# Column-tiled modulation matmuls: four narrow ones per weight row block, or one of 512 columns

## The reference

```python
silu_c = jax.nn.silu(c)            # (1, 1024)
silu_cc = jax.nn.silu(c_ctx)       # (1024,)
for layer in range(DEPTH):         # DEPTH = 2, N_MOD = 6, D = 1024
    mod = (silu_c @ w_mod[layer] + b_mod[layer])[:, None, :]
    mod_c = silu_cc @ w_mod[layer] + b_mod[layer]
    shift1, scale1, gate1, shift2, scale2, gate2 = jnp.split(mod, N_MOD, axis=-1)
```

## Time and profile before

| | before |
|---|---|
| median of 3 runs (lowest, highest) | 2513.5 us (2512.9, 2515.27) |
| the profiled execution's own time | 2513.5 us |
| its span in the profile | 2511.7 us |
| granted TensorE clock, mean share of full speed | 0.996 |
| PE busy | 2447.8 us, 97% |
| ACT busy | 1239.9 us, 49% |
| records of the mod matmuls | 1536 matmuls, 1536 weight loads |
| records of the turns | 24 matmuls, 24 weight loads |

### The profile page before, as it was taken

How to read it: one execution, slowest core, us unless ns; L and a number is a source line. 1 busy time by engine, 2 the same in 40 slices (tenths; PEclk the granted TensorE clock), 3 DMA queues, 4 the chain that set the end, 5 groups by cost and what they waited for, 6 DMA issues and landing times.

```text
span 2511.7 us, 43973 instructions
## 1 busy us (share of the span) xinstructions
PE 2447.8 (97%) x17556; PEld 2170.5 (86%) x17556; DVE 1159.2 (46%) x2116; ACT 1239.9 (49%) x2133; POOL 1462.1 (58%) x853
## 2 busy tenths in 40 slices
PE   7999999999999999999999999999999999999998
PEld 7998889999999889999677877778888878899998
DVE  8896645443978554527426522221001023535144
ACT  6458554455447764446544522453323345636543
POOL 6875747457976755556442334645565546564970
PEclk9999999999999999999999999999999999999999
DMA  6544343345544443346321112232222223245554
GB/s 244 185 168 166 121 168 142 145 185 188 184 168 166 152 174 129 135 156 222 147 71 63 52 68 88 84 117 88 97 101 84 101 107 129 85 152 185 185 185 151
DMA packets 50607, 347.73 MB, mean 138 GB/s; under 512 B 5361, under 2 KB 8689, under 8 KB 8945
## 3 DMA queue, kind: packets, MB, share of 16 engines
q1 hardware_dynamic: 47840, 340.31, 37.3%
q10 hardware_dynamic: 2576, 4.72, 0.6%
HBM read 343.96 MB, written 1.05 MB: 137 GB/s over the span
## 4 chain that ended last, share of the span: by engine, by line
PE 85%; ACT 5%; DVE 4%; POOL 3%; issue 1%; DMA 1%; ACTq 0%; DVEq 0%; SPq 0%; POOLq 0%
PE pg L1951 23%; PE pg L1953 22%; PE pg L1952 22%; POOL ring_lo L668 2%; ACT ring_hi L797 2%; PE ps L2272 2%; PE ps L2293 2%; PE ps L2291 1%; PE ps L2428 1%; PE ps L2409 1%; PE ps L2122 1%; DMA ring<-in_w_stream_dram 1%; PE ps L2128 1%; PE ps L2509 1%; PE ps L2502 1%
## 5 line engine op out<-in xcount | busy, mean ns | idle before, releaser
L668 POOL TENSOR_TENSOR ring_lo<-ring,ring_hi 128x1024 fp32r<-128x1024 f32 (+3 forms) x502 | 1171.2, 2348 | 683.4 <-ACT ring_hi L797 682.7
L1951 PE MATMUL pg<-HH,ring_hi 128*128 128x256 f32 (+1 forms) x3264 | 1036.0, 317 | 15.0 <-POOL ring_lo L668 8.6
L1952 PE MATMUL pg<-HH,ring_lo 128*128 128x256 f32 (+1 forms) x3264 | 989.6, 303 | 0.0
L1953 PE MATMUL pg<-HL,ring_hi 128*128 128x256 f32 (+1 forms) x3008 | 917.7, 305 | 0.0
L1951 PEld LDWEIGHTS pg<-HH,ring_hi 128*128 128x128 f32 x3264 | 616.4, 189 | 72.5 <-issue 33.9
L1952 PEld LDWEIGHTS pg<-HH,ring_lo 128*128 128x128 f32 x3264 | 616.6, 189 | 42.4 <-issue 15.5
L1953 PEld LDWEIGHTS pg<-HL,ring_hi 128*128 128x128 f32 x3008 | 567.7, 189 | 28.1
L797 ACT ACTIVATE ring_hi<-ring 128x1024 fp32r<-128x1024 f32 (+3 forms) x572 | 563.8, 1002 | 35.4 <-DMA ring<-in_w_stream_dram 34.3
L807 ACT ACTIVATE take<-pg 128x256 f32<-128x256 f32 (+1 forms) x242 | 103.7, 429 | 427.2 <-PE pg L1953 421.1
L1953 PE MATMUL pg<-big_r,ring_hi 128*128 128x256 f32 (+1 forms) x928 | 299.4, 323 | 0.0
L1951 PE MATMUL pg<-big_r,ring_hi 128*128 128x256 f32 (+1 forms) x752 | 246.1, 327 | 3.9 <-DVE ring_lo L1637 2.7
(11 more groups left out here) (346 smaller groups left out, 3295.3 us busy)
## 6 DMA issues: line engine op xcount, KB each, us to landing
ring<-in_w_stream_dram SPq DMA_DIRECT2D x320, 1024.0 KB, 4.8
hn<-in_consts_dram ACTq DMA_DIRECT2D x2, 1024.0 KB, 5.8
cst<-in_consts_dram SPq DMA_DIRECT2D x1, 1472.0 KB, 19.9
prm<-in_params_dram SPq DMA_DIRECT2D x1, 1110.0 KB, 9.4
X<-in_xT_dram SPq DMA_DIRECT2D x1, 1024.0 KB, 5.8
X<-in_ctxT_dram ACTq DMA_DIRECT2D x1, 1024.0 KB, 6.4
out_dram<-H ACTq DMA_DIRECT2D x4, 256.0 KB, 2.2
cst<-in_consts_dram SPq DMA_DIRECT2D x1, 768.0 KB, 16.9
```

Of the source, the lines that this page charges most:

```text
L668: pool.tensor_tensor(ring_lo[:, slot, cols], ring[:, slot, cols], ring_hi[:, place * P:(place + n) * P].bitcast(F32), SUB).then_inc(sem(LO ...
L1951: first = pe.matmul(out, a[0], b[0], start=start, stop=False)
L1952: pe.matmul(out, a[1], b[0], start=False, stop=False)
L1953: return first, pe.matmul(out, a[0], b[1], start=False, stop=stop)
```

## The change

Each block of a mod chunk becomes one matmul of 512 columns instead of four of 128. Block c goes to output partitions 32 (c mod 4) and up, so each of the four groups of array columns sums two of the eight blocks, and the sum over the groups is left open. ACT copies the whole 128x512 bank to `mod_rows`. The turn becomes four float32 matmuls, each with 128 columns of `mod_rows` as stationary operand and a new 128x2 constant `sel` as moving operand, which has a one wherever the partition modulo 32 is 0 (first column) or 1 (second column): it sums the four groups and turns the rows at once, so ACT then drains 8 adjoining columns. `n_parts`, `ORDER`, the gaps, the banks and the rings stay as they are. `sel` adds two columns to the early constants.

```diff
+    c["sel"] = (i[:, None] % MOD_COLS == np.arange(2)[None, :]) * 1.0
...
-           "ident": P, "ones": P, "eps6": 1, "eps5": 1, "half_pi": 1, "lam_init": DEPTH, "inv1": 1,
+           "ident": P, "ones": P, "eps6": 1, "eps5": 1, "half_pi": 1, "lam_init": DEPTH, "inv1": 1, "sel": 2,
...
@@ drain_fill (ACT)
-                        act.activation(mod_rows[:, i % 2, 0:P], ready(CHUNK[name, l, i])[:, 0:P], ACT.Copy).then_inc(sem("drained"), 1)
+                        act.activation(mod_rows[:, i % 2, :], ready(CHUNK[name, l, i]), ACT.Copy).then_inc(sem("drained"), 1)
                     elif name == "modt":
-                        columns = ready(CHUNK[name, l, i])[:, 0:P].rearrange("p (a n) -> p a n", a=MOD_TILES)
-                        act.activation(mod[:, l, 4 * i:4 * i + 4, :], columns[:, :, 0:2], ACT.Copy).then_inc(sem("drained"), 1)
+                        drain(CHUNK[name, l, i], mod[:, l, 4 * i:4 * i + 4, :].rearrange("p a b -> p (a b)"), n=8)
@@ chunk_parts (PE)
                     elif name == "mod":
-                        columns = tile(4)
-                        for q in range(MOD_TILES):
-                            ins = pe.matmul(pg[q * MOD_COLS:(q + 1) * MOD_COLS, j % 4, 0:P], sc[:, c, :], columns[:, q * P:(q + 1) * P],
-                                            start=c == 0, stop=c == k - 1)
+                        part = slice(c % MOD_TILES * MOD_COLS, (c % MOD_TILES + 1) * MOD_COLS)
+                        ins = pe.matmul(pg[part, j % 4, :], sc[:, c, :], tile(4), start=c < MOD_TILES, stop=c >= k - MOD_TILES)
@@ turn_rows (PE)
-                pe.transpose(pg[:, j % 4, 0:P], mod_rows[:, i % 2, 0:P], ident).then_inc(sem("chunk_ready"), 1)
+                for q in range(4):
+                    ins = pe.matmul(pg[:, j % 4, 2 * q:2 * q + 2], mod_rows[:, i % 2, q * P:(q + 1) * P], C("sel"), start=True, stop=True)
+                ins.then_inc(sem("chunk_ready"), 1)
```

## The result

| | before | after |
|---|---|---|
| median of the runs side by side | 2513.2 us (4 runs, 2511.19 to 2515.27) | 2531.72 us (4 runs, 2530.24 to 2534.68) |
| ratio, 95% interval | | 1.0072 [1.006, 1.0084] |
| span of the profiled execution | 2511.7 us | 2528.5 us |
| PE records | 17556 | 16572 |

The change makes the kernel 18.5 us, 0.7%, slower (15 to 21 us by the interval); between the two profiled executions lie 16.8 us. The median of all 25 executions of the changed kernel on record is 2530.85 us. PE issues 984 matmuls fewer and is busy for 23 us more.

A forecast was written before the change was run, and what follows sets the result against it. PE, busy for 97% of the span and 85% of the last-ending chain, bounds the kernel. Stretches 5.0, turns 8.8 and ACT 1.1 add +14.9 to 2513.5, giving 2528.5 us; range 2517 to 2543 us.

The forecast's parts named there:

- The stretches: Uninterrupted runs of mod matmuls on PE: those of two or six blocks leave groups idle; +5.3 us, +5.0 after waits.
- p = 0.43 and the overlap: A 512-column pass on one column group takes 0.43 us, and the four groups run side by side.
- The turn: Eight records per chunk on PE instead of one transpose: +0.74 us each, +17.8 us over 24.
- Its cover: PE waits hide part of the turns' +17.8 us: 7.5 behind 15 turns, 1.5 in the gates; +8.8 left.
- the gates' turns: The turn of each layer's gates, claimed hidden whole by PE's later 2.0 us wait for POOL; 1.5 us.
- ACT: Mod drain grows from 266 to 597 ns, 7.9 us over 24; +1.1 us on the path.
- Slots come free at the same blocks, at most 0.4 us later: Ring slots freed by PE's mod blocks: release at most 0.4 us later, with no cost in the sum.
- The sum: Stretches 5.0, turns 8.8 and ACT 1.1 make +14.9 us on 2513.5: 2528.5 us, 0.6% slower.
- the faster groups (p under 0.29): Rival: mod passes on column groups stream faster, p = 0.214, giving 2505 us; chance 0.05.
- passes in order: Rival: a block's second pass holds back the next block, 2579 us, 0.06; with no overlap at all 2645 us, 0.03.
- The cheap turn: Rival: eight turn passes no dearer than the transpose, 2519.6 us; 0.15 together with better cover.
- Delays did spread: Rival: longer ACT drains hold up splits for POOL and a wait grows, up to 2544 us; chance 0.09.

The follow-up runs named there:

- e8: The changed kernel with all eight blocks on group 0, drain and turn reading its 32 partitions: 2634.6 us, 1.0478 of the kernel before.
- e4: The changed kernel with each chunk cut into two parts of four blocks instead of four parts of two: 2527.5 us, 1.0056 of the kernel before.
- e6: The changed kernel with each block as two 256-column matmuls on two groups, and a turn of four records: 2513.39 us, 1.0 of the kernel before.
- e1: The kernel before with only the turn changed to eight records, reading the old 128 columns: 2522.62 us, 1.0036 of the kernel before.
- e3: The changed kernel with ACT draining 128 columns as before, which all four turn matmuls read: 2530.75 us, 1.0063 of the kernel before.
- e11: The kernel before with 32 bytes of padding behind the constants, shifting the later buffers: 2510.01 us against 2512.87, 0.9991.
- e7: The kernel before with the two columns of the constant sel added, unused: 2513.74 us, 1.0 of the kernel before.
- e12: The two-halves kernel (256-column matmuls on two groups) with 32 bytes of padding more behind the constants: 2513.09 us, 1.0001 of the kernel before.

## Why the prediction was right

The forecast was 2528.5 us with a range from 2517 to 2543, slower with 0.85; it came to 2531.72. Its steps in order:

- *The stretches*, +5.3 us, less 0.36 hidden. Right in mechanism and size. With the distances read above, -0.03 x 14, -0.013 x 8, +0.39 x 4 and +0.41 x 12 make +6.0. The whole chunk gained 0.03 and not 0.08: the prediction gave the slower first round (+0.02 to 0.03) to the old form alone, but the new one has it too (the second round starts at 0.453 us, the later ones 0.43 apart), and the old rounds are 0.109 us and not 0.110. Their cover was as forecast: the step at 346.92 us is 0.23 in place of 0.41, the 0.18 that were given. The distances in e4 and e6 show that the cut into parts decides.
- *p = 0.43 and the overlap*. Right; e8 shows both. The rule of the Trainium skill ("TensorE: Matmul & The Clock Gate", Part 3; it stands under "The mechanism", ahead of the section that the prediction names), that a weight load overlaps running matmuls only in another row group, doesn't hold here: loads of column groups that share all rows ran beside passes of 512 columns, 16 passes in 1.92 us against 7.05 in one group.
- *The turn*, +0.70 to +0.79 each, 0.74 taken. It is 0.70, the lower bound: the records follow at 0.10 and not at 0.11 us. 24 times that is 16.8 and not 17.8.
- *Its cover*, 9.0 of 17.8. Right: e1 alone measured +9.0 (5.8 to 12.3) where the prediction's terms give 8.8, and with 0.70 each 7.8. But the gates' turns are not "hidden whole": 0.57 us of each stays on the path (1.1 in all), as e1's trace shows in both layers, since a result of DVE comes later behind them. And what covers the rest isn't the wait for XL, which stayed at 3.9 us over two times, but the wait for POOL's low parts, 1.38 us before and 0.68 now in the second layer. In the first it is gone altogether, because a stretch at the lower clock at 234 us adds 1.5 us there that the wait takes up as well.
- *ACT*, +1.1 on the path of 7.9. Right within what can be told: e3 gives 1.1 back, two medians with intervals of 3 us each, and the rows of the gates' wait show 0.7 of it.
- *"Slots come free at the same blocks, at most 0.4 us later"*, and costed at nothing. This step failed. They come 0.6 us later, by as much as the block on which the signal rides ends later (its last pass starts at 0.45 us and takes 0.59, where it started at 0.15 and took 0.27), and in two places PE waits for what that slot brings: +0.73 and +0.64.
- *The sum*, +14.9. With +1.4 for the two waits, +0.7 for the stretches' size, -1.0 for the turn and +1.1 for the gates' turns it is 17.1, and the traces have 16.8. The lower clock nearly cancels between these two: its places at 42 and 264 us of before stand against those at 862 and 1152 of after, and the wait at 239 us takes up the one at 234. The median has +18.5, whose interval begins at 15. Part of that may be the clock, which the prediction put at nothing without saying so: the mean granted clock is 0.9951 over the 25 executions of the changed kernel and 0.9969 over the 66 of the kernel before that the experiments were compared with, an estimated 9 us more at the lower level. Were none of it hidden by waits, that would cost 4 us, of which the two profiled executions show next to nothing.

Of the rivals, the faster groups (p under 0.29) and passes in order are excluded by e8 and by the 1.92 us of a whole chunk. The cheap turn is excluded by the 0.93 us; the Trainium skill's some 60 cycles for a matmul of few columns ("TensorEngine Tiling (Array Packing)", "Instruction Overhead") is not what the rows show where each has a load of its own, 0.10 us apart. Delays did spread, but only in the two places and behind the gates. The forecast of the time owes a little to luck: the turn was taken 1.0 us too dear, against 3.2 that were left out or taken too small.

## What to carry to other kernels

Column groups run side by side at any length tried here, so a wide matmul on one group costs nothing more in a whole chunk, and 0.98 us in place of 0.57 in a piece of two blocks, which doesn't fill the groups: cut fillers so that each piece fills them, as the halves do. Fewer instructions won nothing, since PE's time went by columns and by weight loads. When an instruction gets longer, look which signals ride on its end: the buffer that it frees comes free later by as much as that instruction ends later (0.6 us here), even if the chunk as a whole ends at the same time.

## What the runs showed of the hardware

**Where operands lie changes the pace of passes.** Moving the buffers behind the constants by 32 bytes (e11) changed the distance between full-array passes of the split products: 120 ns instead of 116 to 122 (median 117) for 256 columns, 226 or 227 instead of 232 to 236 for 512. The plain float32 matmuls did not change. Groups of 512 columns between 1750 and 1950 us (busy, mean ns), of e11 and then of the kernel before:

```profile
L1952 PE MATMUL pg<-HH,ring_hi 128*128 128x512 f32 x206 | 80.1, 389 | 0.0
```

```profile
L1951 PE MATMUL pg<-HH,ring_hi 128*128 128x512 f32 x199 | 78.7, 396 | 0.0
```

In the same 200 us are 206 matmuls instead of 199. The stages of 256 columns lose most of what those of 512 win, and the whole is 0.1% faster, with an interval that reaches to no change. e6's profile has the same mean of 389. Which operand and which address decide wasn't settled.

**The lower clock in short stretches.** The granted clock is 1.00 (2.4 GHz) nearly everywhere, but each of the profiled executions has three to seven places, besides its end, where it is 1.2 GHz for 3.4 us, at some of them for twice that. PE by window (busy (records), clock, DMA share, GB/s), of e7:

```profile
1146.00:1149.00 3.00, 1.32 (x8) 1.00 0.23 93
1149.00:1152.40 3.40, 3.40 (x18) 0.50 0.00 0
```

Ahead of this one PE had waited 2.42 us for ACT, until 1147.68. Passes of 256 columns then started 0.21 us apart instead of 0.12, and the stretch cost about 1.5 us. The profiled execution of before has four such places (42, 264, 612 and 2308 us), that of after five (234, 616, 862, 1152 and 2326), all behind waits of PE, of 0.4 to 3.2 us. They are not all the same places from one execution to the next, and e7's span is 2.3 us longer than that of before with nothing but an unused constant added: two profiled spans can differ by a few us with no cause in the code. How much of an execution lies at the lower clock goes with the code in these runs, though: e3, with the wide matmuls and the long turns, has a mean granted clock of 0.9944 over five runs, and the 21 runs of the kernel before beside it have 0.9966. It doesn't always reach the time: e12 has 0.9954 and is as fast as the kernel before.
